# One 8 KB row per expert slot instead of two 4 KB rows, with the routing in pieces

## What is computed

```python
def block(xc):
    q = (xc @ wq).reshape(c, PEER_HEADS, 2, PEER_HALF)
    s1 = jnp.einsum('chd,kd->chk', q[:, :, 0], k1)
    s2 = jnp.einsum('chd,kd->chk', q[:, :, 1], k2)
    v1, i1 = lax.top_k(s1, PEER_TOPK)
    v2, i2 = lax.top_k(s2, PEER_TOPK)
    cand = (v1[..., :, None] + v2[..., None, :]).reshape(c, PEER_HEADS, PEER_TOPK * PEER_TOPK)
    sc, ci = lax.top_k(cand, PEER_TOPK)
    ia = jnp.take_along_axis(i1, ci // PEER_TOPK, axis=-1)
    ib = jnp.take_along_axis(i2, ci % PEER_TOPK, axis=-1)
    expert = ia * PEER_KEYS + ib
    gate = jax.nn.softmax(sc, axis=-1)
    a = jnp.einsum('chkd,cd->chk', u_tab[expert], xc)
    wgt = gate * jax.nn.gelu(a, approximate=False)
    return jnp.einsum('chk,chkd->cd', wgt, v_tab[expert])
```

## Time and profile before

| | us |
|---|---|
| median of three runs | 1936.28 |
| lowest and highest | 1922.37, 1939.23 |
| span of the profiled execution | 1932.6 |

### The profile page before, as it was taken

One profiled execution on the slowest core, in us unless ns is written; L12 is line 12 of the kernel. 1 busy time (PEld: TensorE's weight loads), 2 busy tenths in 40 slices (PEclk: granted clock), 3 DMA queues, 4 the chain that ended last, 5 costly groups with the idle time before them and its releaser, 6 DMA issues.

```text
span 1932.6 us, 14654 instructions
## 1 busy us (share of the span) xinstructions
PE 1477.8 (76%) x4385; PEld 627.3 (32%) x4385; DVE 1073.3 (56%) x2669; ACT 372.7 (19%) x891; POOL 1271.4 (66%) x1303
## 2 busy tenths in 40 slices
PE   7096478697959977777997776789867777777789
PEld 3055256242314422222442222234322222222233
DVE  4932441486785884445499444447964444444430
ACT  1023223102212211111221111112211111111111
POOL 2902820067777677777777777777777777777773
PEclk9598668899989989999998999999999999999999
DMA  7004407179999899999999999999999999999996
GB/s 304 16 24 89 139 26 319 39 247 321 342 351 381 301 346 402 410 408 409 410 336 346 361 374 372 404 410 362 347 353 374 388 410 408 409 409 409 409 402 231
DMA packets 171053, 618.32 MB, mean 320 GB/s; under 512 B 19728, under 2 KB 25184, under 8 KB 169984
## 3 DMA queue, kind: packets, MB, share of 16 engines
q0 software_dynamic: 156928, 571.18, 77.3%
q1 hardware_dynamic: 14048, 46.22, 7.0%
HBM read 610.52 MB, written 5.19 MB: 319 GB/s over the span
## 4 chain that ended last, share of the span: by engine, by line
PE 24%; DMA 19%; POOL 16%; DVE 15%; issue 7%; ACT 1%; DVEq 0%; ACTq 0%
PE sb_peer_acc L1540 19%; DMA sb_kept_V<-peer_v,sb_kept_expert 17%; POOL sb_peer_U L1180 9%; POOL sb_kept_V L1189 7%; DVE sb_peer_U L1346 4%; PE sb_peer_pq L1465 4%; DMA sb_peer_U<-peer_u,sb_kept_expert 1%; DVE sb_peer_hot L1281 1%; DVE sb_peer_f L1284 1%; DVE sb_peer_idx L1233 1%; DVE sb_peer_idx L1225 1%; DVE sb_peer_left L1226 1%; DVE sb_peer_val L1230 1%; DMA sb_peer_U<-peer_u,sb_peer_es 1%; DVE sb_peer_hot L1283 1%
## 5 line engine op out<-in xcount | busy, mean ns | idle before, releaser
L1540 PE MATMUL sb_peer_acc<-sb_kept_V,sb_peer_dg 128*128 128x512 f32 (+1 forms) x2176 | 1051.9, 619 | 311.7 <-DMA sb_kept_V<-peer_v,sb_kept_expert 205.1
L1346 DVE CUSTOM_DVE_ANT_0 sb_peer_U<-sb_peer_U,sb_rows_xn 128x1024 f32<-128x1024 f32 x512 | 619.6, 1223 | 546.4 <-DMA sb_peer_U<-peer_u,sb_kept_expert 536.7
L1540 PEld LDWEIGHTS sb_peer_acc<-sb_kept_V,sb_peer_dg 128*128 128x128 f32 (+1 forms) x2176 | 380.9, 189 | 958.5 <-issue 504.2
L1189 POOL DMA_INDIRECT sb_kept_V<-peer_v,sb_kept_expert x512 | 550.2, 1075 | 168.8 <-issue 93.5
L1180 POOL DMA_INDIRECT sb_peer_U<-peer_u,sb_kept_expert x512 | 522.2, 1020 | 185.0 <-issue 151.1
L1422 ACT ACTIVATE sb_peer_dg<-sb_kept_ident,sb_peer_wt 128x128 f32<-128x128 f32 (+1 forms) x544 | 210.6, 395 | 1069.8 <-PE sb_peer_acc L1540 841.4
L1180 POOL DMA_INDIRECT sb_peer_U<-peer_u,sb_peer_es x32 | 43.0, 1344 | 142.5 <-DVE sb_peer_es L1285 122.2
L1465 PE MATMUL sb_peer_pq<-sb_rows_wq,sb_peer_xnT 128*128 128x512 f32 x256 | 114.2, 599 | 1.1 <-ACT sb_peer_xnT L1374 1.1
L459 PE MATMUL sb_proj_pz<-sb_proj_w_in,sb_proj_xT 128*128 128x512 f32 (+1 forms) x192 | 73.4, 544 | 8.1 <-DVE sb_proj_xT L317 8.1
L1465 PEld LDWEIGHTS sb_peer_pq<-sb_rows_wq,sb_peer_xnT 128*128 128x128 f32 x256 | 49.0, 192 | 63.8 <-issue 62.3
L459 PEld LDWEIGHTS sb_proj_pz<-sb_proj_w_in,sb_proj_xT 128*128 128x128 f32 x192 | 37.9, 200 | 42.7 <-issue 41.1
(11 more groups left out here) (259 smaller groups left out, 1079.3 us busy)
## 6 DMA issues: line engine op xcount, KB each, us to landing
sb_peer_U<-peer_u,sb_kept_expert POOLq DMA_INDIRECT x512, 6.6
sb_kept_V<-peer_v,sb_kept_expert POOLq DMA_INDIRECT x512, 6.6
sb_proj_w_in<-w_in SPq DMA_DIRECT2D x8, 640.0 KB, 10.7
sb_kept_V<-w_out SPq DMA_DIRECT2D x1, 4096.0 KB, 13.3
sb_proj_xT<-xT SPq DMA_DIRECT2D x8, 272.0 KB, 9.6
sb_proj_x<-x_tok SPq DMA_DIRECT2D x4, 512.0 KB, 12.4
sb_proj_w_mem<-w_mem SPq DMA_DIRECT2D x1, 2048.0 KB, 19.7
sb_blend_MT<-sb_rows_wq SPq DMA_DIRECT2D x8, 256.0 KB, 10.0
```

The lines of the kernel that those rows point to most:

```text
L1189: pool.indirect_dma_start(V[:, m % RV, :], None, d["peer_v"], bass.IndirectOffsetOnAxis(ap=rows(m), axis=0)).then_inc(s_v[m % RV], 16)
L1346: dve.tensor_tensor_reduce(U[:, n % RU, :], U[:, n % RU, :], x, 1.0, 0.0, ALU.mult, ALU.add, a[:, g % 2, n % GRP:n % GRP + 1]).then_inc(s_ ...
L1540: mm = pe.matmul(acc[:r, c, :], dg[:, n % RD, 0:r], V[:, n % RV, c * 512:(c + 1) * 512], start=(s == 0), stop=(s == count[k] - 1))
```

## The change

The host lays u and v of an expert side by side, as one row of 8 KB. One indirect fetch per slot brings 128 such rows into one ring of eight places of 8 KB, so a place is freed only by the slot's matmul. w_out lies in places 0 to 3; slots start at place 4, and fetch 4 waits for the end of all projections. The copies of the sample rows (`xs`) go to `K.xn` itself. Gelu and weight are made for one slot at a time on ScalarE, right after the dot. The routing is cut into twelve pieces, one ahead of each of twelve successive dots; a part's query is likewise cut into four pieces of two products. All four projections, and all norms of ScalarE, stand ahead of the loop. The sums of successive tiles alternate between two halves of `acc`.

```diff
-        RU, RV, RD = 7, 8, 4
-        GRP = TOPK
+        RW, RD, RC = 8, 4, 8
+        WO_SLOTS = 4
...
+        def slot(n):
+            return (n + WO_SLOTS) % RW
...
-        LAG = 34
-        WEIGH = LAG - 1
-        TURN_OUT = 2
-        ROWS_OUT, QTURN, QUERY_OUT, SCORE, EXPS, ROUTE, GATES = 3, 4, 7, 8, 22, 50, 62
-        query = {(1, b): 8 * (b - 1) for b in range(1, 4)}
-        query.update({(k, b): first[k - 1] + 6 + 8 * b for k in range(2, NT) for b in range(4)})
...
-        RESIDUAL, LAST_NORM = (26, 30, 34), 3
-        RESULT = LAG + 2
+        AHEAD = 38
+        QTURN, SCORE, CHUNK = 6, 10, 13
+        ROWS_OUT, QUERY_OUT, EXPS, GATES = 5, 8, CHUNK + 9, CHUNK + 12
+        TURN, TURN_OUT, RESULT = 72, 74, 4
+        query = {(k, b): max(0, first[k] + 32 * b - AHEAD) for k in range(1, NT) for b in range(4)}
...
+        def sums_in(k):
+            return acc[:, 2 * (k % 2):2 * (k % 2) + 2, :]
...
-        out_banks = [acc[:, :, :], acc[:, :, :], acc[:, :, :], psc[:, 2:4, :], psc[:, 0:2, :]]
+        out_banks = [acc[:, 0:2, :], acc[:, 2:4, :], acc[:, 0:2, :], pq[:, :, :], acc[:, 2:4, :]]
...
-                for n in range(NS + LAG):
...
+                for n in range(NS):
                     k, s = steps[n]
+                    at = K.expert[:, order[k], s:s + 1] if k else es[:, s:s + 1]
+                    if s % QS == 0:
+                        pool.wait_ge(s_id, part(k, s // QS) + 1)
+                    if n == RW - WO_SLOTS:
+                        pool.wait_ge(s_om, NT)
+                    if n >= RW:
+                        pool.wait_ge(s_mm, n - RW + 1)
+                    pool.indirect_dma_start(rows[:, slot(n), :], None, d["peer_uv"],
+                                            bass.IndirectOffsetOnAxis(ap=at, axis=0)).then_inc(s_uv[slot(n)], 16)
...
-                def route(k, b):
-                    best(k, b)
-                    sums(k, b)
-                    numbers(k, b)
...
+                def route(k, b, c):
+                    if c == 0:
+                        best_first(k, b)
+                    elif c < 3:
+                        best_taken(k, b, c - 1)
...
+                    else:
+                        numbers_key(k, b, c - 10)
...
+                    if n < 3:
+                        residual(2 + n)
+                        norm(2 + n)
+                    if k and s == RESULT:
+                        result(k - 1)
+                    for c in range(12):
+                        for kb in due(n, CHUNK + c):
+                            route(*kb, c)
                     for kb in due(n, GATES):
                         gates(*kb)
...
+                    dve.wait_ge(s_uv[slot(n)], 16 * (n // RW + 1))
+                    u = rows[:, slot(n), 0:D]
+                    dve.tensor_tensor_reduce(u, u, K.xn[:, order[k], :], 1.0, 0.0, ALU.mult, ALU.add,
+                                             a[:, n % RC:n % RC + 1]).then_inc(s_dot, 1)
...
+                for k in range(1, NT):
+                    norm(k)
                 turned_out(1)
...
+                    if s % QS == 0:
+                        act.wait_ge(s_gt, part(k, s // QS) + 1)
+                    act.wait_ge(s_dot, n + 1)
+                    act.activation(ga[:, c:c + 1], a[:, c:c + 1], ACT.Gelu).then_inc(s_ga, 1)
+                    gate = K.gate[:, order[k], s:s + 1] if k else gs[:, s:s + 1]
+                    act.wait_ge(s_ga, n + 1)
+                    act.activation(wt[:, c:c + 1], ga[:, c:c + 1], ACT.Copy, scale=gate).then_inc(s_wt, 1)
                     if n >= RD:
                         act.wait_ge(s_mm, n - RD + 1)
...
+                    act.wait_ge(s_wt, n + 1)
+                    act.activation(dst, src, ACT.Copy, scale=wt[:, c:c + 1]).then_inc(s_dg, 1)
...
-                def queries(k, b):
+                def queries(k, b, c2):
...
+                    for c in (2 * c2, 2 * c2 + 1):
                         mm = pe.matmul(pq[:r, 0, :], xnT[:, c, 0:r], K.wq[:, c, 4 * b * P:4 * (b + 1) * P],
...
-                project(1)
+                for j in range(1, NT):
+                    project(j)
                 turn(1)
-                queries(1, 0)
-                turn_queries(1, 0)
-                scores(1, 0)
-                for j in range(2, NT):
-                    project(j)
...
+                    pe.wait_ge(s_uv[slot(n)], 16 * (n // RW + 1))
+                    if n == 0:
+                        pe.wait_ge(s_h, 3)
+                    if n == first[1]:
+                        pe.wait_ge(s_h, 5)
...
+        K.rows = S.sb("rows", [P, 8, 2 * D])
+        K.wo = K.rows[:, 0:4, :].rearrange("p a (b c) -> p (a b) c", c=D)
...
-        "peer_u": A["peer_u"][0],
-        "peer_v": A["peer_v"][0],
+        "peer_uv": np.concatenate([A["peer_u"][0], A["peer_v"][0]], 1),
```

More of the change, by code:

```diff
@@ L963, in gate @@
         bg = S.sb("bg", [P, 4])
-        yT = S.sb("yT", [P, 4, CH, COLS])
+        room = K.rows[:, 4:8, :].rearrange("p a b -> p (a b)")
+        yT = room[:, 0:4 * CH * COLS].rearrange("p (k t j) -> p k t j", k=4, t=CH)
         sg = S.sb("sg", [P, 2, 4, COLS])
@@ L1119, in experts @@
         s_gt = S.sem("gates_known")
-        s_u = [S.sem(f"u_landed{n}") for n in range(RU)]
-        s_v = [S.sem(f"v_landed{n}") for n in range(RV)]
+        s_uv = [S.sem(f"rows_landed{n}") for n in range(RW)]
         s_dot = S.sem("dots")
@@ L1209, in residual, with norm @@
                     ins.then_inc(s_h, 1)
+                def norm(k):
+                    i = order[k]
+                    r = ROWS[i]
                     dve.wait_ge(s_std, k + 1)
@@ L1272, in numbers, with numbers_column @@
                     step(dve.scalar_tensor_tensor(F[1], F[0], -64.0, F[1], ALU.add, ALU.max))
+                def numbers_column(k, b):
+                    r, n = held[k], QS
+                    F = [f[:r, m, 0:n] for m in range(4)]
                     ts(F[2], F[1], 1.0, 8.0, ALU.min, ALU.mult)
@@ L1321, in _ @@
                 gates(0, 0)
                 residual(1)
[L1323 removed]
+                norm(1)
+                dve.wait_ge(s_xs, 48)
                 for n in range(NS):
                     k, s = steps[n]
[L1326 to L1335 removed]
+                    if n < 3:
[3 more added lines that the diff above has]
+                        result(k - 1)
+                    for c in range(12):
+                        for kb in due(n, CHUNK + c):
+                            route(*kb, c)
@@ L1336, in _ @@
                     for kb in due(n, GATES):
                         gates(*kb)
-                    if k and s == RESULT:
-                        result(k - 1)
-                    if n == ROUTE0:
-                        route(1, 0)
-                    for kb in due(n, ROUTE):
-                        route(*kb)
-                    dve.wait_ge(s_u[n % RU], 16 * (n // RU + 1))
-                    x = K.xn[:, order[k], :] if k else xs[:, :]
-                    dve.tensor_tensor_reduce(U[:, n % RU, :], U[:, n % RU, :], x, 1.0, 0.0, ALU.mult, ALU.add,
-                                             a[:, g % 2, n % GRP:n % GRP + 1]).then_inc(s_dot, 1)
@@ L1526, in _ @@
                     r = ROWS[order[k]]
-                    if k and k + 1 < NT and s == 0:
+                    if k and k + 1 < NT and s == TURN:
                         turn(k + 1)
-                    for kb in due(n, 0):
-                        queries(*kb)
+                    for c2 in range(4):
+                        for kb in due(n, c2):
+                            queries(*kb, c2)
                     for kb in due(n, QTURN):
@@ L1535, in _ @@
                     pe.wait_ge(s_dg, n + 1)
-                    pe.wait_ge(s_v[n % RV], 16 * (n // RV + 1))
-                    if k and s == 0:
-                        pe.wait_ge(s_y, k)
-                    for c in range(2):
-                        mm = pe.matmul(acc[:r, c, :], dg[:, n % RD, 0:r], V[:, n % RV, c * 512:(c + 1) * 512],
+                    pe.wait_ge(s_uv[slot(n)], 16 * (n // RW + 1))
[3 more added lines that the diff above has]
+                        pe.wait_ge(s_h, 5)
+                    if k >= 2 and s == 0:
+                        pe.wait_ge(s_y, k - 1)
+                    for e in range(2):
+                        mm = pe.matmul(sums_in(k)[:r, e, :], dg[:, n % RD, 0:r], rows[:, slot(n), D + e * 512:D + (e + 1) * 512],
                                        start=(s == 0), stop=(s == count[k] - 1))
```

184 lines of the change are left out of this document (80 added, 104 removed).

## The result

The changed kernel takes **1804.09 us** (median; 1803.43 to 1804.38) against 1932.22 for the kernel before in the same session: a ratio of 0.9349, 95% interval 0.9301 to 0.9396. The profiled execution took 1804.31 us with a span of 1802.5. The forecast was 1819 within 1795 to 1880.

What follows compares the result with a forecast made beforehand. The DMA engines were taken as the bound, near 409 GB/s, with losses at routing, GpSimd issue, start and tail. 446.1 + 1356.6 + 4.1 + 8.5 = 1815, plus 3.7, gave 1819 us; own range 1795 to 1845, eight in ten 1795 to 1880.

Steps and rivals of the forecast that it cites:

- outside the span: Added to the sum: 3.7 us by which the median of the kernel before exceeded its profiled span.
- The slot's DMA time: Moving one slot's 128 rows of u and v takes 2.55 us, between 2.515 and 2.56.
- GpSimd's fetch: One 8 KB-row fetch per slot occupies GpSimd 0.94 to 1.1 us, at most 2.29 with issue and dot wait, staying hidden.
- The rival that it goes by bytes: GpSimd's fetch lengthens with bytes: 3.23 us per slot, 2180 us in total; all slower outcomes together got 0.07.
- the reading of the kernel before: Gather loses 148 us: start 26, routing stretches 44 plus 34, GpSimd-issue stretches some 24, tail 20.
- Routing pieces hidden: Twelve routing pieces on VectorE, 14.3 us per routing, cost nothing under cover of the fetch; 229 us without cover.
- Ring and queries: Slot loop of 11.2 us, 16.1 with VectorE and TensorE lags, fits eight slots' 20.4 us; the queue stays full.
- ScalarE: Gelu, Copy and diagonal per slot take 1.0 of 2.55 us, hidden; tables load about once per Exp.
- The start: DMA stands from 394 to fetch 4 at 421.5; fetch 11 goes out at 440.4, lands at 446.1; 31 us lost.
- The tail: The end is one slot's chain of dot, ScalarE, matmul, result and store: 8.5 us.
- the dry queue: Rival: queue runs dry at each query and routing, 64 us more, 1883; with routing loss kept, chance 0.14.
- the 64 KB rate for large rows: Rival: large rows move at the rate of 64 KB packets, 417 GB/s, 19 us less: 1800; no separate chance given.

Runs made afterwards that it cites:

- run 1: Changed kernel with only the merging of u and v undone, two fetches of 4 KB rows per slot: 1914.73 us, ratio 0.9906 to the kernel before.
- Run 2: Kernel before with one edit, its routing cut into twelve pieces, two ahead of each of six dots: 1903.64 us, ratio 0.9874.
- run 5: Changed kernel with all twelve routing pieces of a part standing again ahead of one dot: 1904.18 us.
- Run 7: Changed kernel with six ring slots in use instead of eight: 1815.69 us.
- run 4: Changed kernel with two fetches of 4 KB rows per slot and each dot replaced by a copy of one column: 1836.62 us.
- run 3: Changed kernel with each dot replaced by a copy of one column, still one fetch of 8 KB rows per slot: 1799.59 us.
- the variant with eighths and earlier projection: Changed kernel with a part's query in eight pieces in successive steps and three chunks of the first prompt tile's projection moved earlier: 1796.31 us.

## Why the prediction was right

Its sum set against the trace:

| term | forecast us | measured us |
|---|---|---|
| slot 11 in the ring | 446.1 | 450.8 (start of its dot) |
| 532 slots, with the stores | 1356.6 + 4.1 = 1360.7 | 1793.9 - 450.8 = 1343.1 |
| from the last dot's start | 8.5 | 8.6 |
| outside the span | 3.7 | 1.8 |

*The slot's DMA time was mis-sized.* I took 2.55 us, near the 4 KB row, between bounds of 2.515 and 2.56 that I thought safe. In calm stretches it is 2.49, as between these two dots:

```profile
1781.57 1.23 DVE L1353 CUSTOM_DVE_ANT_0 sb_kept_rows<-sb_kept_rows,sb_rows_xn 128x1024 f32<-128x1024 f32 x1 [1.25 <-DMA sb_kept_rows<-peer_uv,sb_kept_expert]
...
1784.06 1.22 DVE L1353 CUSTOM_DVE_ANT_0 sb_kept_rows<-sb_kept_rows,sb_rows_xn 128x1024 f32<-128x1024 f32 x1 [1.25 <-DMA sb_kept_rows<-peer_uv,sb_kept_expert]
```

The "upper" rate of 417 GB/s was the mean of a window from 298 to 318 us that the transfer did not fill. In the kernel before it was issued only inside it:

```profile
298.32 0.34 SPq L616 DMA_DIRECT2D sb_rows_wq<-wq  x1
```

The same 8.34 MB in the 19.68 us that are left make 424 GB/s, so 417 was no upper bound. Over all 532 slots it came to 1343.1/532 = 2.525 with stores, dips and a late end (last section), 17.6 us less than forecast. That is more than the whole error of 14.7 (1819 against the profiled 1804.3): the start gave 4.7 back, and 1.9 less lay outside the span. Of the 4.7, 2.1 lie ahead of the stage, whose first product starts at 344.18 us instead of 342.12; most of the rest is fetch 11, which takes 8.2 us from its issue to its dot where 5.7 were forecast.

The Trainium skill ("DMA: Bandwidth & Descriptors", SWDGE vs HWDGE vs iDMA) prefers packets of up to 4096 bytes from GpSimd. Here the queue of the fetches makes 78592 packets, half of the 156928 that run 1 shows, and from 700 to 720 us all but the small ones are of 8 KB:

```profile
DMA packets 1157, 8.43 MB, mean 422 GB/s; under 512 B 128, under 2 KB 128, under 8 KB 128
```

The 8 KB row stays whole, and fetching so is faster, 422 against 409 GB/s. The measurement decides.

*GpSimd's fetch* was right: 0.94 to 1.1 us forecast, 1.074 measured, and the bytes don't count. The rival that it goes by bytes is out.

*The step that failed was the reading of the kernel before*, though the sum didn't show it. I had laid 78 us of its 148 lost ones to routing and 24 to GpSimd. Run 2 gives back 29. The rows for a better reading were there: I counted GpSimd's busy time plus 0.30 us per instruction for 1080 to 1210 only. For the stretch "of routing", 446 to 720, the same sum is 205.10 + 179 x 0.30 = 259 of 274 us, and for the whole gather 1151.02 + 1088 x 0.30 = 1477 of 1548. GpSimd had 15 us over where I had the routings lose 44, and even in the calm stretch of 409 GB/s, 244.08 + 250 x 0.30 = 319 of 320, it was as full as DMA. So it had next to nothing left to make up for a stop. I also passed over the strip's lowest slice but the last, 301 GB/s in slice 13, when I wrote 336 to 374. The total came out right because the change takes away both causes at once, and I summed up to DMA's rate rather than by causes; of either edit alone the same reading would have been wrong, as runs 1, 2 and 5 show. That it did no harm here is luck.

*Routing pieces hidden*: right, and the cover was priced too high: 229 us without it was forecast, 100 measured with the block whole (run 5), since the ring takes part of a block.

*Ring and queries*: "the queue stays full" holds to within 9 us (419 against 422 GB/s). Run 7 fits the estimate of 11.2 to 16.1 us for the loop.

*ScalarE*: hidden, and the tables were loaded once per Exp and once back (17 each), not once per Gelu, as forecast. What I had missed is in the last section.

*The start*: fetch 4 at 423.59 and fetch 11 at 442.67 us, 421.5 and 440.4 forecast; DMA empty from 395 to 421, as told. *The tail*: 8.6 for 8.5.

*Rivals*: the dry queue cost 9 us in all, not 64; the 64 KB rate for large rows (1800) was the nearest of them, with 422 GB/s measured and 424 in the window above.

## What to carry to other kernels

Before laying a loss to the block that is seen, add up each engine's busy time plus its gap per instruction in that very stretch: an engine that is full there will keep the time when the block goes, and two such causes are worth little one by one and much together. A bound from a transfer of another shape holds only if its window was full from end to end. When the stream runs at its rate, look for the rest at its two ends.

## What the runs showed of the hardware

Without dots the gather goes from 409 GB/s (two fetches of 4 KB rows per slot, run 4) to 422 (one of 8 KB rows, run 3), and an indirect fetch takes GpSimd the same time for either, 0.944 to 0.949 us. Beside dots it grows: 1.07 on average and 1.99 at most in the changed kernel.

One DMA engine ends late. The last stretches of the gather in the changed kernel:

```profile
1784.00:1786.00 2.00, 1.90 (x4) 0.59 (x4) 1.23 (x2) 0.55 (x3) 0.00 (x0) 1.00 0.95 397
1786.00:1788.00 2.00, 1.60 (x4) 0.68 (x4) 1.23 (x2) 0.55 (x2) 0.00 (x0) 1.00 0.29 119
1788.00:1790.00 2.00, 1.51 (x4) 0.65 (x4) 1.02 (x1) 0.70 (x3) 0.00 (x0) 1.00 0.06 25
1790.00:1792.00 2.00, 1.54 (x5) 0.47 (x4) 0.76 (x3) 0.90 (x3) 0.00 (x0) 1.00 0.07 29
```

From 1788 on the DMA share is 0.06 to 0.07, one engine of sixteen, at 25 to 29 GB/s (a sixteenth of 422 is 26), while the dots still come every 2.4 to 2.5 us until 1793.92. The share of 0.29 from 1786 to 1788 puts the end of the other fifteen at about 1786.5, some three slots ahead. An estimate from these rows: shared by all sixteen, the rest would end about 7 us sooner. The second trace of the changed kernel shows the same. Why one engine lags was not tried.

A table switch on ScalarE stands ahead of one dip of DMA. Order of time in the variant with eighths and earlier projection, and the stretches behind it:

```profile
1263.88 1.28 ACT L1419 ACT_TABLE_LOAD   x1
...
1266.25 10.55 PE L1549 MATMUL sb_peer_acc<-sb_kept_rows,sb_peer_dg 128*128 128x512 f32 x20 [1.89 <-ACT sb_peer_dg L1427]
```

```profile
1268.00:1270.00 2.00, 2.00 (x4) 0.86 (x3) 1.97 (x5) 0.02 (x1) 0.56 (x1) 0.50 1.01 422
1270.00:1272.00 2.00, 2.00 (x6) 0.81 (x5) 1.54 (x5) 1.20 (x5) 0.84 (x2) 0.86 1.03 360
1272.00:1274.00 2.00, 2.00 (x6) 0.86 (x5) 1.23 (x2) 0.95 (x4) 1.23 (x2) 1.00 0.86 336
```

The Exp with a load ahead of it and this one behind it holds up one Gelu, TensorE waits 1.89 us instead of 0.5, its clock stands at 0.50 (1.2 GHz) from 1268 to 1270, and DMA dips to 336 GB/s some four us later. But the last two pieces of a routing stand on VectorE in the same steps and delay the dots too. Cutting those pieces and moving the Exp moved the dips and gained nothing, so the order of these rows is shown; the cause of the dip and its price are not.
